# Expert weights requested and multiplied gate first, then up; the shared product inside the expert loop; a last pair that gathers nothing

## The reference

```python
def routed_moe(hn, w_router, router_bias, we_gate, we_up, we_down, ws_gate, ws_up, ws_down):
    scores = sigmoid(t @ w_router)                        # 64 experts
    _, idx = lax.top_k(scores + router_bias, TOP_K)       # 8 of 64 for each token
    gates = ...                                           # normalised scores of the chosen, times 2.5
    a = einsum('td,edf->tef', tb, we_gate)                # 1024 -> 256 in each expert
    b = einsum('td,edf->tef', tb, we_up)
    hid = silu(a) * b * gb[..., None]
    routed = einsum('tef,efd->td', hid, we_down)          # 256 -> 1024
    shared = (silu(hn @ ws_gate) * (hn @ ws_up)) @ ws_down
    return routed + shared
```

## Time and profile before

| | |
|---|---|
| median of 3 runs | 921.95 us (921.51 to 922.22) |
| the profiled execution's own time | 922.21 us |
| its span, first to last instruction | 920.4 us |
| TensorE busy | 895.9 us, 97% |
| DVE / ACT / POOL busy | 499.8 / 197.9 / 46.1 us |
| HBM read | 263.69 MB, 289 GB/s over the span |
| granted TensorE clock | 0.999 of full |

### The profile page before, as it was taken

How to read it: one execution, slowest core, us unless ns; L and a number is a source line. 1 busy time by engine, 2 the same in 40 slices (tenths; PEclk the granted TensorE clock), 3 DMA queues, 4 the chain that set the end, 5 groups by cost and what they waited for, 6 DMA issues and landing times.

```text
span 920.4 us, 17072 instructions
## 1 busy us (share of the span) xinstructions
PE 895.9 (97%) x7204; PEld 447.4 (49%) x7204; DVE 499.8 (54%) x933; ACT 197.9 (22%) x398; POOL 46.1 (5%) x72
## 2 busy tenths in 40 slices
PE   8999999999999999999999999999999999999998
PEld 7888755455745554465344344344343333333344
DVE  3656726945577886873534544444443434343447
ACT  2314100122426550251111111111111111101022
POOL 4011100040200000020000000000000000000000
PEclk9999999999999999999999999999999999999999
DMA  8634326454052258678999999999999999999921
GB/s 259 221 137 139 136 92 202 137 187 157 27 182 92 93 182 343 263 275 310 403 422 422 422 422 422 422 422 422 423 422 422 422 422 422 422 422 422 412 95 47
DMA packets 66030, 266.04 MB, mean 289 GB/s; under 512 B 11289, under 2 KB 13962, under 8 KB 41034
## 3 DMA queue, kind: packets, MB, share of 16 engines
q1 hardware_dynamic: 65978, 265.54, 73.2%
q10 hardware_dynamic: 16, 0.00, 0.0%
HBM read 263.69 MB, written 1.84 MB: 289 GB/s over the span
## 4 chain that ended last, share of the span: by engine, by line
PE 77%; DMA 15%; SPq 3%; DVE 3%; ACT 1%; issue 1%; POOL 0%; DVEq 0%; ACTq 0%; POOLq 0%
PE bank L1411 17%; PE bank L950 15%; DMA arena<-in_we_up 14%; PE bank L1059 9%; PE bank L940 9%; PE bank L1438 7%; PE bank L1370 3%; PE bank L1383 3%; SPq L513 3%; PE bank L1486 2%; PE bank L927 2%; PE bank L1013 2%; PE bank L1314 1%; PE bank L1154 1%; PE bank L1427 1%; PE bank L1333 1%
## 5 line engine op out<-in xcount | busy, mean ns | idle before, releaser
L1411 PE MATMUL bank<-arena 128*32 128x512 f32 x2048 | 225.9, 593 | 12.5 <-DMA arena<-in_we_up 11.5
L1411 PEld LDWEIGHTS bank<-arena 128*32 128x32 f32 x2048 | 67.2, 110 | 167.0 <-issue 152.3
L950 PE MATMUL bank<-arena 128*128 128x512 f32 x264 | 117.8, 598 | 0.0
L1438 PE MATMUL bank<-arena 128*32 128x512 f32 x1024 | 116.5, 595 | 0.0
L1059 PE MATMUL bank<-actT,arena 128*128 128x256 f32 x384 | 85.3, 380 | 0.0
L940 PE MATMUL bank<-arena,actT 128*128 128x512 f32 x192 | 83.5, 593 | 0.0
L1059 PEld LDWEIGHTS bank<-actT,arena 128*128 128x128 f32 x384 | 72.0, 190 | 10.2 <-issue 0.8
L950 PEld LDWEIGHTS bank<-arena 128*128 128x128 f32 x264 | 48.8, 190 | 57.8 <-issue 57.6
L2089 DVE SCALAR_TENSOR_TENSOR arena<-arena,gslot,bank 128x256 f32<-128x256 f32 x32 | 15.4, 480 | 108.5 <-ACT arena L889 108.5
L889 ACT ACTIVATE arena<-bank 128x256 f32<-128x256 f32 x32 | 12.3, 384 | 269.3 <-PE bank L1411 268.7
L674 ACT ACTIVATE arena<-bank 128x512 f32<-128x512 f32 (+2 forms) x69 | 35.5, 534 | 154.5 <-PE bank L940 82.7
(11 more groups left out here) (318 smaller groups left out, 913.9 us busy)
## 6 DMA issues: line engine op xcount, KB each, us to landing
arena<-in_we_gate SPq DMA_DIRECT2D x32, 2048.0 KB, 24.7
arena<-in_we_up SPq DMA_DIRECT2D x32, 2048.0 KB, 29.2
arena<-in_we_down SPq DMA_DIRECT2D x32, 2048.0 KB, 28.0
arena<-in_w_in SPq DMA_DIRECT2D x17, 2048.0 KB, 8.3
arena<-in_w_branch_gdn SPq DMA_DIRECT2D x2, 2048.0 KB, 7.7
arena<-in_w_branch_fox SPq DMA_DIRECT2D x2, 2048.0 KB, 8.5
arena<-in_w_out SPq DMA_DIRECT2D x2, 2048.0 KB, 9.8
arena<-in_w_ple_gate SPq DMA_DIRECT2D x2, 2048.0 KB, 32.5
```

Source lines behind the costliest of these rows:

```text
L950: ins = t.matmul(o[:, :], lhs[:, c, :], rhs[:, c, :], start=fresh and c == 0, stop=c == HC - 1, skip_group_check=not fresh)
L1411: ins = t.matmul(bank[4][i * CAP:i * CAP + CAP, :], xg[:, c, i * CAP:i * CAP + CAP], w, start=(c == 0), stop=(c == KC - 1))
L1438: ins = t.matmul(bank[4 + j][i * CAP:i * CAP + CAP, :], hidT[:, c, i * CAP:i * CAP + CAP], d_in[s][:, i % 2, c * D + WT * j:c * D + WT * j ...
```

## The change

Four things change. Gate and up weights get semaphores of their own (`gate_loaded`, `up_loaded`) and TensorE makes two products of them, first all of gate (ended by the new `pgate_filled`), then all of up (ended by `pgu_filled`); SP requests the next gate weights of a slot after the first and the up weights after the second. The shared down product is divided by token tiles, one behind pair 6, one behind pair 12; the loop becomes three loops of two, two and six turns. The last pair has no gathering and no places, neither on TensorE nor on DVE and ACT (they now stand at the head of a second pass, with the step of `iota`). And DVE's `shared_hidden(0)` stands ahead of the last subtraction of `rest_of_parts(1)`. ACT's loop has one pair in its body where it had two.

```diff
             def load_pair(s, pick, done):
+                sp.wait_ge(pgate_filled, done)
+                load_gate(s, pick)
                 sp.wait_ge(pgu_filled, done)
-                load_gate_up(s, pick)
+                load_up(s, pick)
                 sp.wait_ge(y_filled[1], done)
                 load_down(s, pick)
...
             def pair(s, prev, before, turn, e2, splits, columns=None):
-                pe.wait_ge(gu_loaded[s], turn * 32)
+                pe.wait_ge(gate_loaded[s], turn * 16)
                 pe.wait_ge(xa_ready, before + 1)
                 pe.wait_ge(xb_ready, before + 1)
                 pe.wait_ge(y_ready[0], before + 1)
-                for c in range(KC):
-                    for i in range(2 * NT):
-                        w = gu_in[s][:, :, i % 2, c * DE:c * DE + DE]
-                        ins = t.matmul(bank[4][i * CAP:i * CAP + CAP, :], xg[:, c, i * CAP:i * CAP + CAP], w, start=(c == 0), stop=(c == KC - 1))
-                ins.then_inc(pgu_filled, 1)
+                for m, done in enumerate((pgate_filled, pgu_filled)):
+                    if m == 1:
+                        pe.wait_ge(up_loaded[s], turn * 16)
+                    for c in range(KC):
+                        for i in range(2 * NT):
+                            ins = t.matmul(bank[4][i * CAP:i * CAP + CAP, m * DE:m * DE + DE], xg[:, c, i * CAP:i * CAP + CAP],
+                                           gu_in[s][:, m, i % 2, c * DE:c * DE + DE], start=(c == 0), stop=(c == KC - 1))
+                    ins.then_inc(done, 1)
...
-                gather(before + 2)
+                if e2 is not None:
+                    gather(before + 2)
                 pe.wait_ge(phidT_ready, before + 1)
-                places(e2)
+                if e2 is not None:
+                    places(e2)
                 pe.wait_ge(d_loaded[s], turn * 16)
                 for j in range(2):
-                    if j == 1:
+                    if j == 1 and e2 is not None:
                         pe.wait_ge(xa_ready, before + 2)
...
-            all_but_last(0, shared_columns)
+            first_pair(0, shared_columns)
+            triples(0, 0, 2)
             pe.wait_ge(sdw_loaded, 16)
-            for n in range(NT):
-                shared_down(n)
+            shared_down(0)
+            triples(0, 2, 4)
+            shared_down(1)
+            triples(0, 4, PAIRS // SLOTS)
             last_pair(0)
...
                 seq(v.tensor_copy(hparts[:, 1, n, :], hn[:, n, :]))
+                if n == 1:
+                    shared_hidden(0)
                 v.tensor_tensor(hparts[:, 2, n, :], hn[:, n, :], hparts[:, 1, n, :], ALU.subtract).then_inc(parts_ready, 1)
...
             place_tokens(slice(0, 2))
             rest_of_parts(1)
-            shared_hidden(0)
             shared_hidden(1)
...
+                last = r * PAIRS + (PAIRS - 1)
+                hidden(last)
+                dve.wait_ge(spread_made, last)
+                v.tensor_copy(spread_last, spread[1]).then_inc(last_spread, 1)
+                output(last)
```

More of the change, by code:

```diff
@@ L883, in _, with hidden, output, experts @@
             act.wait_ge(passes_ready, 1)
[L884 to L894, removed]
+            np_act = act.value_load(passes[0:1, 0:1], min_val=1, max_val=P // CAP)
+            def hidden(t):
+                act.wait_ge(pgu_filled, t)
+                a.activation(sil, bank[4][:, 0:DE], ACT.Silu).then_inc(psilu, 1)
+                act.wait_ge(phidT_filled, t)
+                a.activation(hidT, bank[7][:, 0:DE].rearrange("p (c t) -> p c t", c=2), ACT.Copy).then_inc(phidT_ready, 1)
+            def output(t):
+                act.wait_ge(y_filled[0], t)
+                a.activation(y[:, 0:WT], bank[4][:, :], ACT.Copy).then_inc(y_ready[0], 1)
+            def experts(r):
+                with act.Fori(0, PAIRS - 1) as k:
+                    hidden(r * PAIRS + k + 1)
+                    gathered(r * PAIRS + k + 2)
+                    output(r * PAIRS + k + 1)
+                hidden(r * PAIRS + PAIRS)
+                output(r * PAIRS + PAIRS)
+            experts(0)
+            with act.If(np_act > 1):
+                with act.Fori(1, np_act) as r:
+                    gathered(r * PAIRS + 1)
+                    experts(r)
             for n in range(NT):
-                act.wait_ge(added, np_act * 2 + (2 * n + 2))
+                act.wait_ge(added, np_act * PAIRS + (2 * n + 2))
                 a.activation(hsum[:, n, WT:D], bank[2 * n + 1][:, :], ACT.Copy).then_inc(hsum_right, 1)
@@ L1440, in pair, with triples @@
                     ins.then_inc(y_filled[j], 1)
-            def all_but_last(r, columns=None):
-                pair(0, None, r * PAIRS, r * TURNS[0] + 1, slice(2, 4), r, columns)
-                with pe.Fori(0, PAIRS // SLOTS) as k:
+            def triples(r, lo, hi):
+                with pe.Fori(lo, hi) as k:
                     for i in range(1, SLOTS + 1):
@@ L2084, in _, with hidden @@
             np_dve = dve.value_load(passes[0:1, 0:1], min_val=1, max_val=P // CAP)
-            def pair(following, before, e2, splits=None):
+            def hidden(before):
                 dve.wait_ge(psilu, before + 1)
@@ L2090, in pair, with take @@
                                        scalar=gslot[:, 0:1], in1=up, op0=ALU.mult, op1=ALU.mult).then_inc(phid_ready, 1)
+            def take(following, before):
                 dve.wait_ge(xb_filled, before + 2)
@@ L2098, in pair, with output @@
                 v.tensor_reduce(gslot[:, :], gpart[:, :], AX.X, ALU.add).then_inc(place_ready, 1)
[L2099 to L2102, removed]
+            def output(before):
                 dve.wait_ge(y_filled[1], before + 1)
                 v.tensor_copy(y[:, WT:D], bank[5][:, :]).then_inc(y_ready[1], 1)
-                if splits is None:
-                    return
+            def pair(following, before, e2, splits):
+                hidden(before)
+                take(following, before)
+                place_tokens(e2)
+                output(before)
                 dve.wait_ge(y_ready[0], before + 2)
@@ L2115, in pair, with experts @@
                 v.tensor_tensor(yparts[:, 2, :], y, yparts[:, 1, :], ALU.subtract).then_inc(y_split, 1)
-            with dve.Fori(0, np_dve) as r:
+            def experts(r):
                 pair(1, r * PAIRS, slice(4, 6), r * (PAIRS - 1))
@@ L2122, in _ @@
                              r * (PAIRS - 1) + k * SLOTS + i)
[L2123 to L2126, removed]
+                last = r * PAIRS + (PAIRS - 1)
[3 more added lines that the diff above has]
+                output(last)
+            experts(0)
+            with dve.If(np_dve > 1):
+                with dve.Fori(1, np_dve) as r:
+                    dve.wait_ge(onehot_ready, r * PAIRS + 2)
+                    v.tensor_scalar(iota[:, :], iota[:, :], float(CAP), None, ALU.add).then_inc(iota_moved, 1)
+                    dve.wait_ge(iota_moved, r)
+                    take(0, r * PAIRS - 1)
+                    place_tokens(slice(2, 4))
+                    experts(r)
             for n in range(NT):
```

24 lines of the change are left out of this document (18 added, 6 removed).

## The result

| | before | after |
|---|---|---|
| median | 921.46 us (11 runs, 920.75 to 923.07) | 916.70 us (11 runs, 913.73 to 919.00) |
| the profiled execution, its span | 922.21, 920.4 | 914.95, 913.1 |
| TensorE busy | 895.9 | 894.1 |

The ratio is 0.9943 (0.9934 to 0.9952): faster by 4.8 us, where 13.7 were forecast, and outside the range. The runs also lie further apart than before, over 5.3 us; at a mean granted clock of 0.998 or 0.999 they took 913.7 to 916.1, at 0.996 916.3 to 917.2, at 0.994 917.1 to 919.0.

What follows compares the result with a forecast made beforehand. The weight stream was the bound, 1.2 us a pair slower than TensorE. Stream 3.7 us earlier (1.05 + 2.6), shared product off the end and a shorter last pair: closing product at 878.0, -13.7 us, 908.5 us; range 905.8 to 914.

Steps and rivals of the forecast that it cites:

- Step 5: Last pair without gathering: down product 0.9 us earlier, closing product possible at 877.7, waiting 0.3 for weights landing at 878.0.
- step 3: Separate gate and up requests: gate slots asked for 3.45 us earlier per pair, saving 2.6 us of stream (0 to 4.0).
- step 1: DVE's shared product moved ahead of the last subtraction: TensorE's first pair and the requests hanging on it 1.05 us earlier.
- Step 4: Shared down product in halves inside the loop: its 7.06 us leaves the end, using time TensorE would wait for the stream.
- Rival B: First requests win less: only 1.05 us left, closing weights land at 880.6, 911.1 us; chance 0.12.
- second hole: Stream gap at pair 3's down weights (452.4 us), said to cost 1.3 of the 5.0 us lost at the start.
- Step 2: Two products of 256 columns for one of 512: +0.04 us a pair, 1.3 in all.
- D: Small overhead per matmul group in gate/up products: 222 ns a group, 0.2 us a pair, 913 us; chance 0.08.
- E: One weight load per group no longer hidden: 1.05 us a pair, 941 us, slower than before; chance 0.04.
- first hole: Stream gap at 432 to 436 us, only 129 GB/s, said to cost 3.7 of the 5.0 us lost.
- Rival C: TensorE's longer loop body isn't kept; seven back edges wait for fetches, 1 us each shown, 915 us; chance 0.14.

Runs made afterwards that it cites:

- two_tails: The changed kernel with TensorE's closing part written twice, once directly behind the last pair, so nothing is jumped over before it: 911.19 us, ratio 0.9883.
- no_early: `two_tails` with DVE's `shared_hidden(0)` back behind the parts, as before the change: 912.18 us, ratio 0.9895.
- no_halves: `two_tails` with the shared down product whole behind one loop of ten turns: 914.27 us, ratio 0.9916.
- gather_alone: The changed kernel with only the last pair's missing gathering kept, all other parts undone: 921.31 us, ratio 0.9994.
- late_closing: The changed kernel with the closing weights requested only once the last pair's output is done: 922.59 us, a single execution.
- no_pass: The changed kernel without TensorE's code for a second pass, so nothing is jumped over: 911.44 us, ratio 0.989.

## Why the prediction was wrong

The forecast of the closing product's start was 878.0; the profile of after has 884.5. The gap is 6.5 us. Along TensorE it is 2.4 of stream (the up product at 865.0, not 862.6) and 4.4 behind the down product, less the 0.3 that the forecast had the closing product wait for its weights. Against `two_tails`, which has no stall, it is 2.9 for closing weights that land late (880.9, not 878.0) and 3.6 for the jump (884.5 - 880.9); in medians 2.7 (911.19 - 908.5) and 5.5 (916.70 - 911.19). The stream's part alone would have left the time inside the range; the jump takes it out:

- **Step 5, the end, failed** (5.5 us in the medians). It ran TensorE from the down product straight into the additions, "closing product possible at 877.7", and priced no branch between them. The idle there is 3.86 where `two_tails` has 0.86, and the addition takes 3.48 for 2.08. In before the fetch fell into 882 to 887 us, with the closing weights down since 881.7; the down product's start and that landing could be read from the earlier trace rows. By moving the jump 11.6 us forward the change put it into those transfers.
- **The stream's forecast failed too** (2.4 us at the last up weights), and mostly behind the part that step 3 reckoned with. 2.6 of the 5.0 lost microseconds and the 1.05 of step 1 were to bring the stream forward by 3.7. Pair 4's down weights land at 465.8 and not 468.6, which is 2.9; the six kernels that are alike up to there have 464.3 to 466.0, so 3.7 lies within what executions differ by. But the last up weights come only 1.3 earlier (865.0, not 866.3): 1.6 us go in the stretch with the further loops (384.3 for 382.7), most of it in the step at 566.6. Step 4 put the cost of these loops on the stream at nothing. Rival B, closing weights at 880.6 and 911.1 us, is what `two_tails` gave (880.9 and 911.2), by another mechanism than it named.
- **The "second hole"** of 1.3 us in before was misread. It is the landing step of 6.3 at 463.6, of up weights that had been asked for at 448.6, while the weights two before them were still coming (452.4); the request behind them started at 454.83, so the queue never ran empty and earlier requests could not save it. (A slip without weight: the transfers of before are full from the twenty-first slice on, not from the nineteenth, which has 310 GB/s.)
- **Step 1** was right: the product at 419.24, no idle at L1345, the gathering 1.39 earlier (423.64 to 422.25). Whether this reaches the end is open (`no_early`).

```profile
419.24 0.42 DVE L2074 TENSOR_TENSOR arena<-arena,bank 128x256 f32<-128x256 f32 x1
...
419.88 0.59 PE L1345 MATMUL bank<-arena,identb 128*128 128x512 bf16 x2
...
422.25 1.56 PE L1393 MATMUL bank<-onehot,arena 128*128 128x64 bf16 x48
```

- **Step 2** was right: 6.91 us a product, 13.72 a pair. Rivals D and E needed 222 and 231 ns a group; 216 came (6.91 / 32). The Trainium skill's 60 cycles for each matmul (TensorEngine Tiling (Array Packing), Instruction Overhead) don't show here.
- **Step 3's first hole** did close. 432 to 436 us carried 129 GB/s and now:

```profile
432.00:436.00 4.00, 3.98 (x61) 2.50 (x62) 0.48 (x1) 1.69 (x4) 0.00 (x0) 1.00 0.96 401
```

- **Step 4** was right in its balance: stream and TensorE are level (3 waits left). What the halves save wasn't the 7.06 that stood at the end but 3.1: part of the time that they free goes into waiting for up and closing weights, and the two extra loops cost the stream time, which the step did not price (384.3 us for the same 77 requests in `two_tails`, 382.7 in `no_halves`).
- **Rival C** had the mechanism of the miss, and almost its time (915), but the wrong place. The loop body of 1,344 records is kept, and no back edge shows an idle; the fetch that stalls is at the one jump out. The Trainium skill (Runtime: NRT & Kernel Launch, Instruction fetch mechanics) says that a taken branch out of the window at hand forces a fetch before execution goes on. At the exit jump the trace agrees (3.86 us), at the back edges it doesn't, and that the fetch's price depends on what else is in flight (1.8 to 1.9 us to the packet without weights, 4.7 with them) only the runs tell.

The trace of before could have given the warning. The one instruction packet between the down product and the addition was in it, and TensorE's wait for DVE's copy only just hid the fetch (L1472 started 0.2 us behind the copy); what happens to it beside the closing weights was the question to ask.

## What to carry to other kernels

When an end is made shorter, look at each taken branch in it and at what is in flight at the new time: a jump over code that isn't run was hidden with an idle stream and cost 5 us here with 4 MB on the way. Put the path that is run right behind the work before it, even at the price of writing the closing code twice. And count loops as well as instructions: here the two further loops, whose bodies are fetched anew, took 1.6 us from a weight stream that was the bound.

## What the runs showed that I had not expected

- The price of one instruction fetch: the packet comes 1.8 to 1.9 us behind the start of the work ahead of the jump without other transfers (before, `gather_alone`, `late_closing`), 4.7 us with the closing weights in flow. In the two kernels where TensorE then waited for more than DVE's copy it went on 2.8 us (after) and 3.0 us (`gather_alone`) behind the packet.
- The idle costs twice: 3.9 us of it, and then TensorE at half speed from 878 us until within the window of 880 to 882, which added 1.4 us. It also seems to be why the time scatters: after's eleven runs span 5.3 us, the four of `two_tails` 1.3 and of `no_pass` 1.9. As an estimate from the mean granted clocks, full-speed time of 0.002 x 915 = 1.8 us is missing in the profiled run, 3.7 in the median one (0.996), 5.5 in the slowest (0.994); the first two differ by 1.9, and the times by 1.75.
- A stream that reads 420 to 423 GB/s in every slice can still lose 1.4 us at a landing. It shows in the spacing of the landings (6.4 for 4.97).
